# Two-layer hybrid decoder, one core: the expert loop with the down product one expert later and whole gate and up matrices

## The chip, the cores and the metric

One core of a Trainium2 chip runs the whole program. The metric is the time of one execution in microseconds (us), the median of several runs. A profile of one execution gives the spans, waits and transfers below.

## What is computed

Two layers on x of 512 tokens by 1024 columns, all float32: a mixer (state-space and sparse attention in layer 0, block attention in layer 1), and after each mixer a mixture of experts. The mixture is the part that matters here:

```python
h = rms_norm(x, ffn_norm[i])
# router: one of 4 groups, then 2 of its 8 experts per token; 32 experts
def expert_block(args):
    xblk, e = args
    hid = jax.nn.silu(xblk @ w_gate[e]) * (xblk @ w_up[e])
    return hid @ w_down[e]
y = jnp.zeros_like(xt).at[row_token].add(yb * row_weight[:, None].astype(yb.dtype))
x = x + y
```

Each expert has w_gate and w_up of 1024 x 512 and w_down of 512 x 1024, 2 MiB each, so 6 MiB per expert, 32 experts in each of two layers, 384 MiB in all.

## The kernel before

**The expert loop.** Every expert serves up to 64 tokens (CAP). All 32 experts run in order, whatever the router chose. The five engines each run their own program of the loop (`per_expert`, L2059) and meet at semaphores. For expert c TensorE runs, in this order: `gate_up` (L2016, the products at L1951) in two halves over the rows of the matrices; `x_turn` of expert c+1 (four transposes, L1939); two of three passes that pick the rows of expert c+2 out of the tokens (`pick_begin`, L1924); `hid_turn` (two transposes, L1957); the third pass (`pick_end`); and `down` (L2028, the products at L1964). ScalarE computes the silu (L2043), copies the picked rows (L1935) and copies the result out of PSUM (`y_out`, L2048). VectorE multiplies with the up half (L2053), copies the turned hidden rows (L2057) and applies the norm's gain (L1943). GpSimd scatters each expert's result into y_d in DRAM (L1970). The result of expert 31 is not scattered: TensorE adds it at the end from SBUF (L2278).

**The weights.** Three slots (RING = 3) in SBUF each hold the three matrices of one expert. The sync engine's queue (SP) loads them in `moe_sp` (L2104), and its order is the order of the transfers. A gate or up matrix comes as two halves of 1 MiB (`one_half`, L1894, rows of the program at L1897), four rows (8 KB) to a partition; w_down comes in one transfer of 2 MiB (L1906). For c from 0 to 28 `next_weights` (L2127) loads expert c+3 into the slot of c:

```python
                sp.wait_ge(S(f"{t}_guh"), c + 1 + L * NE)
                half_weights(sp, t, L, c + RING, u, 0)
                sp.wait_ge(S(f"{t}_gu"), c + 1 + L * NE)
                half_weights(sp, t, L, c + RING, u, 1)
                sp.wait_ge(S(f"{t}_dn"), c + 2 + L * NE)
                down_weights(sp, t, L, c + RING, u)
```

The semaphore m_guh says that the first half of gate/up is done, m_gu the second, m_dn the down product.

**The end of a layer.** When the scatters of experts 0 to 30 have landed (`fence`, L2076), SP fetches y_d back in four transfers (L2147). VectorE weighs and adds each (`add_fetched`, L2476), then adds expert 31's part (`add_last`, L2483), which gives x for the next layer, or for the output.

**Ahead of the loop.** The normed tokens are split in three bf16 parts: the high part by ScalarE (`high_part`, L663), the rest by VectorE (`rest_part`, L754), middle and low parts at L760 and L769. The last tile is also kept whole (`norm_last`, L675).

Of the kernel before, what the change touches and what calls it, by code (L numbers as in the profile page):

```python
# [81 lines left out]
RING = 3  # L82
# [116 lines left out]
def build(nc, ins, out):  # L199
    ctx = ExitStack()  # L200
    with ctx:
# [379 lines left out]

        def outproj_pe(pe, att, tag, mixT, wo, L):
# [69 lines left out]
        def outproj_act(act, tag, L):  # L652
# [8 lines left out]
            def high_part(i):  # L661
                act.wait_ge(S("norm_rstd"), NT * ORDER[nt] + i + 1)
                nc.scalar.activation(parts[0][i], xt[:, i, :], ACT.Copy, scale=rstd[:, i:i + 1]).then_inc(S("m_hi"), 1)  # L663
# [11 lines left out]
            nc.scalar.activation(norm_last, xt[:, NT - 1, :], ACT.Copy, scale=rstd[:, NT - 1:NT]).then_inc(S("m_norm_last"), 1)  # L675
# [74 lines left out]
        def rest_part(dve, L, i):  # L750
# [3 lines left out]
            nc.vector.scalar_tensor_tensor(rows[:, i, :], xt[:, i, :], rstd[:, i:i + 1], parts[0][i], ALU.mult,  # L754
                                           ALU.subtract).then_inc(S("m_rest"), 1)
# [1137 lines left out]

        def one_half(sp, t, layer, e, u, n, h):  # L1894

            src = ins[("moe_w_gate", "moe_w_up")[n]][layer, bass.ds(e, 1), h * 512:(h + 1) * 512].rearrange("e (p j) f -> p e (j f)", j=4)
            sp.dma_start(wgu[u][:, n, 4 * h:4 * h + 4].rearrange("p (e j) f -> p e (j f)", e=1), src).then_inc(S(f"{t}_{('wgu', 'wgv')[h]}{u}"), 16)  # L1897

        def half_weights(sp, t, layer, e, u, h):

            for n in range(2):
                one_half(sp, t, layer, e, u, n, h)

# [90 lines left out]
        def pick_begin(pe, t, c):  # L1994
            pe.wait_ge(S(f"{t}_ones"), c + 1)
            pe.wait_ge(S(f"{t}_rows"), c + 1)
            pick_rows(range(2))

        def pick_end(pe, t, c):
            pick_rows(range(2, 3)).then_inc(S(f"{t}_picked"), 1)  # L2000

        def picked(pe, t, c):
            pick_begin(pe, t, c)
            pick_end(pe, t, c)
# [11 lines left out]
        def gate_up(pe, t, c, cu, u):  # L2016
# [4 lines left out]
            pe.wait_ge(S(f"{t}_wgv{u}"), 32 * (cu + 1))  # L2021
# [50 lines left out]

        def uses(u):
# [30 lines left out]
        def moe_sp(sp, L, mixed, att):  # L2104
            t, x = "m", f"mx{L}"
            if L == 0:
                for n in range(2):
                    sp.dma_start(row_gain[:, n], ins["ffn_norm"][n].rearrange("(h p j) -> p h j", h=2, j=4)).then_inc(S("gain_in"), 16)
# [18 lines left out]
            def next_weights(c, u):  # L2127
# [428 lines left out]
```

## Time and profile before

| | us |
|---|---|
| median of 3 runs (lowest, highest) | 1636.38 (1635.76, 1638.82) |
| the profiled execution | 1636.7 |
| its span, first to last instruction | 1634.6 |
| TensorE matmul busy | 1577.5 (97%) |
| VectorE, ScalarE, GpSimd busy | 484.7, 360.8, 197.6 |
| moved by all transfers | 474.21 MB |

The span is what the profile measures between its first and last instruction; the remaining 2.1 us of the profiled execution lie around it. "Busy" of TensorE counts overlapping matmuls once. In the profile's timeline a row gives the start, the length, the engine, the line, the operation and, in brackets, how long the engine stood idle before it and what ended that. SPq is the sync engine's queue; a row there is the issue of a transfer and not its delivery. Layer 0's expert loop begins at 326.6 us, layer 1's at 1155.7 us.

### The profile page before, as it was taken

What the parts mean: (1) busy time and instruction counts of PE and PEld (TensorE: products, weight loads), DVE (VectorE), ACT (ScalarE), POOL (GpSimd) and SP (SyncE); (2) the same over time, 40 slices, a digit from 0 to 9 for tenths busy, and PEclk for the clock granted to TensorE, in tenths of its full rate; (3) what the DMA queues carried; (4) which work ended last, traced back from release to release, by engine and by line L of the source; (5) the groups of instructions that cost most, each with busy time, mean ns of one, the idle gap of its engine ahead of it and who ended that gap; (6) DMA issues with size and microseconds to landing.
All of it is one profiled execution on the core that took longest, in us unless ns stands there. A gap on an engine that the chain in (4) does not pass through costs nothing.

```text
span 1634.6 us, 21323 instructions
## 1 busy us (share of the span) xinstructions
PE 1577.5 (97%) x8068; PEld 738.3 (45%) x8072; DVE 484.7 (30%) x1252; ACT 360.8 (22%) x853; POOL 197.6 (12%) x298
## 2 busy tenths in 40 slices
PE   7999989999999999999799999999999999999995
PEld 4545664543333333333445468855433333333332
DVE  1485851531111111111514125734511111111114
ACT  2354461311111111111200246732111111111110
POOL 2240320000000000000102022420000000000000
PEclk9999999999999999999999999999999999999999
DMA  8620127389999999999933320052899999999997
GB/s 244 258 103 7 54 55 308 124 345 420 423 421 421 422 422 422 422 422 419 353 50 104 142 56 1 2 235 78 345 421 421 421 422 421 422 421 422 422 422 310
DMA packets 118314, 474.21 MB, mean 290 GB/s; under 512 B 40822, under 2 KB 47222, under 8 KB 68333
## 3 DMA queue, kind: packets, MB, share of 16 engines
q1 hardware_dynamic: 110156, 456.98, 69.8%
q10 hardware_dynamic: 3136, 8.40, 1.3%
q0 software_dynamic: 4960, 8.04, 1.3%
q8 instruction: 36, 0.59, 0.2%
q14 instruction: 26, 0.21, 0.0%
HBM read 454.84 MB, written 26.77 MB: 295 GB/s over the span
## 4 chain that ended last, share of the span: by engine, by line
PE 67%; SPq 12%; DMA 4%; DVE 3%; issue 1%; ACT 1%; POOL 0%; DVEq 0%; POOLq 0%
PE bank L1951 19%; SPq L1897 10%; PE bank L1964 9%; PE bank L1543 8%; PE bank L1924 8%; PE bank L597 7%; DMA arena<-in_moe_w_up 3%; PE bank L409 3%; PE bank L444 3%; PE bank L1939 2%; SPq L1906 2%; PE bank L426 2%; PE bank L1957 1%; DVE arena L2476 1%; PE bank L458 1%
## 5 line engine op out<-in xcount | busy, mean ns | idle before, releaser
L1951 PE MATMUL bank<-arena 128*64 128x512 f32 x2048 | 451.4, 592 | 6.3 <-DMA arena<-in_moe_w_up 5.9
L1951 PEld LDWEIGHTS bank<-arena 128*64 128x64 f32 x2048 | 143.6, 137 | 302.1 <-issue 291.0
L1964 PE MATMUL bank<-arena 128*64 128x512 f32 x1024 | 230.6, 592 | 2.1 <-DVE arena L2057 2.1
L2053 DVE TENSOR_TENSOR arena<-arena,bank 128x256 f32<-128x256 f32 x64 | 27.0, 422 | 637.2 <-ACT arena L2043 637.1
L1970 POOL DMA_INDIRECT y_d<-arena,slot_row x62 | 60.7, 979 | 857.9 <-ACT arena L2048 830.7
L1924 PE MATMUL bank<-arena 128*64 128x512 bf16 x1272 | 160.1, 381 | 0.2
L1543 PE MATMUL bank<-arena 128*128 128x512 f32 x320 | 139.1, 593 | 0.8 <-ACT arena L321 0.8
L1964 PEld LDWEIGHTS bank<-arena 128*64 128x64 f32 x1024 | 71.9, 137 | 124.1 <-issue 110.5
L2043 ACT ACTIVATE arena<-bank 128x256 f32<-128x256 f32 x64 | 24.6, 384 | 410.5 <-PE bank L1951 410.5
L597 PE MATMUL bank<-arena 128*128 128x512 f32 x256 | 111.8, 594 | 0.0
L895 PE MATMUL bank<-arena 128*128 128x512 f32 (+1 forms) x288 | 105.3, 525 | 0.0
L1543 PEld LDWEIGHTS bank<-arena 128*128 128x128 f32 x320 | 60.1, 190 | 74.3 <-issue 73.3
L1924 PEld LDWEIGHTS bank<-arena 128*64 128x64 bf16 x1272 | 66.8, 109 | 55.5 <-issue 1.2
L1935 ACT ACTIVATE gain<-bank 128x512 f32<-128x512 f32 x64 | 38.2, 597 | 223.5 <-PE bank L1924 222.2
L2048 ACT ACTIVATE arena<-bank 128x512 f32<-128x512 f32 x64 | 38.3, 599 | 190.4 <-PE bank L1964 190.4
L895 PEld LDWEIGHTS bank<-arena 128*128 128x128 f32 x288 | 49.8, 190 | 54.5 <-issue 54.5
L536 DVE CUSTOM_DVE_ANT_0 arena<-bank,arena 128x512 f32<-128x512 f32 (+3 forms) x128 | 52.3, 415 | 72.4 <-PE bank L409 57.5
L597 PEld LDWEIGHTS bank<-arena 128*128 128x128 f32 x256 | 47.9, 190 | 57.1 <-issue 57.1
L409 PE MATMUL bank<-arena 128*128 128x31 f32 (+8 forms) x256 | 67.0, 396 | 0.9 <-ACT arena L1189 0.9
L444 PE MATMUL bank<-arena 128*128 128x128 f32 x384 | 60.8, 281 | 2.2 <-DVE arena L506 1.7
L1939 PEld LDWEIGHTS bank<-ident,gain 128*128 128x128 f32 x256 | 35.9, 210 | 49.6 <-issue 48.7
L2057 DVE COPY arena<-bank 128x256 f32<-128x256 f32 x64 | 27.2, 425 | 89.2 <-PE bank L1957 88.9
(319 smaller groups left out, 1505.0 us busy)
## 6 DMA issues: line engine op xcount, KB each, us to landing
arena<-in_moe_w_gate SPq DMA_DIRECT2D x128, 1024.0 KB, 20.2
arena<-in_moe_w_up SPq DMA_DIRECT2D x128, 1024.0 KB, 23.0
arena<-in_moe_w_down SPq DMA_DIRECT2D x62, 2048.0 KB, 23.3
arena<-in_even_w_in SPq DMA_DIRECT2D x4, 2048.0 KB, 8.4
y_d<-arena ACTq DMA_DIRECT2D x2, 4096.0 KB, 16.8
arena<-y_d SPq DMA_DIRECT2D x8, 1024.0 KB, 9.3
arena<-bias_row_d SPq DMA_DIRECT2D x2, 3584.0 KB, 11.9
arena<-in_odd_w_in SPq DMA_DIRECT2D x3, 2048.0 KB, 14.2
```

The lines of the kernel that those rows point to most:

```text
L409: mm = nc.tensor.matmul(score_bank[u["a"] % 4][:, 0:u["L"]], u["q"], u["k"], start=True, stop="mask" not in u)
L444: mm = nc.tensor.matmul(bank[4 + u["m"] % 2][:, u["b"] * D:(u["b"] + 1) * D], self.pT[0:w, u["a"] % 2, kt, :], u["v"](kt), start=(kt == 0) ...
L536: ins_ = nc.vector.tensor_tensor_reduce(out=self.p[:, u["a"] % 4, 0:L], in0=score_bank[u["a"] % 4][:, 0:L], in1=u["bias"], scale=-1.0, sca ...
L597: mm = nc.tensor.matmul(mix_bank(n)[:, :], mixT[:, k, i * P:(i + 1) * P], wo[half][:, k, :], start=(k == 0), stop=(k == KD - 1))
L895: mm = nc.tensor.matmul(o, l, r, start=(k == 0), stop=(k == KD - 1))
L1543: mm = nc.tensor.matmul(o, lhs(k), rhs(k), start=(k == 0), stop=(k == KD - 1))
L1897: sp.dma_start(wgu[u][:, n, 4 * h:4 * h + 4].rearrange("p (e j) f -> p e (j f)", e=1), src).then_inc(S(f"{t}_{('wgu', 'wgv')[h]}{u}"), 16)
L1924: mm = nc.tensor.matmul(bank[4][h * CAP:(h + 1) * CAP, :], pick[:, i, :], parts[part][i][:, h * 512:(h + 1) * 512], start=(part == 0 and i ...
L1939: mm = nc.tensor.transpose(bank[0][:, j * P:(j + 1) * P], xe[:, j::4], ident[:])
L1951: mm = nc.tensor.matmul(bank[1][fh * CAP:(fh + 1) * CAP, :], xeT[:, j, half * CAP:(half + 1) * CAP], wgu[u][:, :, n, fh * FH:(fh + 1) * FH ...
L1964: mm = nc.tensor.matmul(bank[3][dh * CAP:(dh + 1) * CAP, :], hidT[:, j, fh * CAP:(fh + 1) * CAP], wd[u][:, n, dh * 512:(dh + 1) * 512], st ...
L1970: return nc.gpsimd.indirect_dma_start(out=y_d[layer][:, :], out_offset=bass.IndirectOffsetOnAxis(ap=slot_row[:, n:n + 1], axis=0), in_=yb[ ...
```

## The change

Three things are changed.

1. TensorE runs the down product of expert c-1 right behind gate/up of expert c, and the three passes of picking are together again (`picked`). For the first expert there is no down product ahead, and expert 30's down product (after == 1) and expert 31's run behind their own hid_turn as before. ScalarE's `y_out` moves along.
2. SP loads gate and up of experts 6 to 29 whole, 2 MiB in one transfer, eight rows (16 KB) to a partition, after m_gu (`whole_weights`). Experts 0 to 5, 30 and 31 keep their halves. The down matrix of expert c+2 is now asked for after the gate and up matrices of expert c+3.
3. So that eight consecutive rows can lie on a partition, the columns of the normed tokens are stored in another order: ScalarE and VectorE read x by `by_cols` and write by `by_rows`; `rest_part` becomes two VectorE instructions of 512 columns instead of one of 1024.

```diff
+        def by_cols(ap):
+            return ap.rearrange("t (p h j) -> t h p j", h=2, j=4)
+        def by_rows(ap):
+            return ap.rearrange("t (h p j) -> t h p j", h=2, j=4)
...
-                nc.scalar.activation(parts[0][i], xt[:, i, :], ACT.Copy, scale=rstd[:, i:i + 1]).then_inc(S("m_hi"), 1)
+                nc.scalar.activation(by_rows(parts[0][i]), by_cols(xt[:, i, :]), ACT.Copy, scale=rstd[:, i:i + 1]).then_inc(S("m_hi"), 1)
...
-            nc.vector.scalar_tensor_tensor(rows[:, i, :], xt[:, i, :], rstd[:, i:i + 1], parts[0][i], ALU.mult,
-                                           ALU.subtract).then_inc(S("m_rest"), 1)
+            for h in range(2):
+                ins_ = nc.vector.scalar_tensor_tensor(by_rows(rows[:, i, :])[:, h], by_cols(xt[:, i, :])[:, h], rstd[:, i:i + 1],
+                                                      by_rows(parts[0][i])[:, h], ALU.mult, ALU.subtract)
+            ins_.then_inc(S("m_rest"), 1)
...
+        def whole_weights(sp, t, layer, e, u):
+
+            for n in range(2):
+                src = ins[("moe_w_gate", "moe_w_up")[n]][layer, bass.ds(e, 1)].rearrange("e (p j) f -> p e (j f)", j=KD)
+                sp.dma_start(wgu[u][:, n].rearrange("p (e j) f -> p e (j f)", e=1), src).then_inc(S(f"{t}_wgu{u}"), 16)
...
-            def next_weights(c, u):
+            def next_weights(c, u, halved):
+                if not halved:
+                    sp.wait_ge(S(f"{t}_gu"), c + 1 + L * NE)
+                    whole_weights(sp, t, L, c + RING, u)
+                    next_down(c - 1, (u - 1) % RING)
+                    return
                 sp.wait_ge(S(f"{t}_guh"), c + 1 + L * NE)
                 half_weights(sp, t, L, c + RING, u, 0)
                 sp.wait_ge(S(f"{t}_gu"), c + 1 + L * NE)
...
                     sp.dma_start(wd[2][:, 3, :], down[1][:, 1]).then_inc(S("m_wdq"), 16)
+                else:
+                    next_down(c - 1, (u - 1) % RING)
+
+            def next_down(c, u):
                 sp.wait_ge(S(f"{t}_dn"), c + 2 + L * NE)
                 down_weights(sp, t, L, c + RING, u)
             for u in range(RING):
-                next_weights(u, u)
+                next_weights(u, u, True)
             with sp.Fori(1, TRIPS - 1) as it:
                 for u in range(RING):
-                    next_weights(it * RING + u, u)
+                    next_weights(it * RING + u, u, False)
             for u in range(NE - RING * TRIPS):
-                next_weights(RING * (TRIPS - 1) + u, u)
+                next_weights(RING * (TRIPS - 1) + u, u, True)
+            next_down(NE - RING - 1, (NE - RING - 1) % RING)
...
             def body(e, c, cu, u, after):
-                gate_up(pe, t, c, cu, u)
-                if isinstance(c, int) and c == L * NE:
+                opening = isinstance(c, int) and c == L * NE
+                gate_up(pe, t, c, cu, u, in_halves(L, e, u))
+                if not opening and after >= 1:
+                    down(pe, t, c - 1, cu - (u == 0) + L * (uses((u - 1) % RING) - uses(u)), (u - 1) % RING)
+                if opening:
...
                 if after >= 1:
                     x_turn(pe, t, c + 1)
-                if after >= 2:
-                    pick_begin(pe, t, c + 2)
                 hid_turn(pe, t, c)
                 if after >= 2:
-                    pick_end(pe, t, c + 2)
+                    picked(pe, t, c + 2)
+                else:
+                    down(pe, t, c, cu, u)
                 if isinstance(c, int) and c == L * NE + 2:
                     pe.wait_ge(S("m_wdq"), 32 * (L + 1))
-                down(pe, t, c, cu, u)
```

**SP's queue at the end of a layer's loads.** Before: w_down of expert 30, then gate and up of expert 31 in halves, then its w_down:

```order
L1906 DMA arena<-in_moe_w_down 128x2x2048 [waits m_dn]
L1897 DMA arena<-in_moe_w_gate 128x2048 [waits m_guh]
L1897 DMA arena<-in_moe_w_up 128x2048
L1897 DMA arena<-in_moe_w_gate 128x2048 [waits m_gu]
L1897 DMA arena<-in_moe_w_up 128x2048
L1906 DMA arena<-in_moe_w_down 128x2x2048 [waits m_dn]
```

After the change, the same place: w_down of expert 29 (L1925), gate and up of expert 31, and then w_down of experts 30 and 31:

```order
L1925 DMA arena<-in_moe_w_down 128x2x2048 [waits m_dn]
L1906 DMA arena<-in_moe_w_gate 128x2048 [waits m_guh]
L1906 DMA arena<-in_moe_w_up 128x2048
L1906 DMA arena<-in_moe_w_gate 128x2048 [waits m_gu]
L1906 DMA arena<-in_moe_w_up 128x2048
L1925 DMA arena<-in_moe_w_down 128x2x2048 [waits m_dn] x2
```

Before, expert 30's down matrix stood ahead of expert 31's gate and up; now it stands behind all four of them.

**TensorE at experts 30 and 31, after the change** (L1970 is gate/up, L1983 the down product, L1958 x_turn, L1976 hid_turn, L2280 the transposes of the last expert's weights; m_wd2, m_wd0 and m_wd1 are the down matrices of experts 29, 30 and 31):

```order
L1970 MATMUL bank<-arena 64x512 [waits m_wgv0]
L1970 MATMUL bank<-arena 64x512 x7
L1983 MATMUL bank<-arena 64x512 [waits m_wd2,m_y,m_hT]
L1983 MATMUL bank<-arena 64x512 x7
L1958 MATMUL bank<-ident,gain 128x128 [waits m_xT,m_rows]
L1958 MATMUL bank<-ident,gain 128x128 x3
L1976 MATMUL bank<-ident,arena 128x128 [waits m_hid]
L1976 MATMUL bank<-ident,arena 128x128
L1983 MATMUL bank<-arena 64x512 [waits m_wd0,m_y,m_hT]
L1983 MATMUL bank<-arena 64x512 x7
L2280 MATMUL bank<-ident,arena 128x128 [waits y_gated]
L1970 MATMUL bank<-arena 64x512 [waits m_wgu1,m_hid,m_xT]
```

Expert 29's down product has moved behind gate/up of expert 30; expert 30's own stands, as before, ahead of gate/up of expert 31.

## Rows read from the trace of the kernel before

**Rows 1.** The page: DMA rate and share in 40 slices of the span.

```profile
DMA  8620127389999999999933320052899999999997
GB/s 244 258 103 7 54 55 308 124 345 420 423 421 421 422 422 422 422 422 419 353 50 104 142 56 1 2 235 78 345 421 421 421 422 421 422 421 422 422 422 310
```

**Rows 2.** The page: costliest group, busy us, mean ns | idle before it, releaser.

```profile
L1951 PE MATMUL bank<-arena 128*64 128x512 f32 x2048 | 451.4, 592 | 6.3 <-DMA arena<-in_moe_w_up 5.9
```

**Rows 3.** Timeline of TensorE, one expert in mid-loop, and the next one's start.

```profile
501.93 7.03 PE L1951 MATMUL bank<-arena 128*64 128x512 f32 x32
...
512.74 3.60 PE L1964 MATMUL bank<-arena 128*64 128x512 f32 x16
...
516.17 7.03 PE L1951 MATMUL bank<-arena 128*64 128x512 f32 x32
```

**Rows 4.** Timeline of TensorE, experts 29 (its down), 30 and 31, layer 0.

```profile
758.37 3.60 PE L1951 MATMUL bank<-arena 128*64 128x512 f32 x16
762.50 3.65 PE L1951 MATMUL bank<-arena 128*64 128x512 f32 x16 [0.53 <-DMA arena<-in_moe_w_up]
...
768.15 3.65 PE L1964 MATMUL bank<-arena 128*64 128x512 f32 x16 [0.55 <-DVE arena L2057]
...
773.13 3.65 PE L1951 MATMUL bank<-arena 128*64 128x512 f32 x16 [0.74 <-DMA arena<-in_moe_w_up]
778.15 3.65 PE L1951 MATMUL bank<-arena 128*64 128x512 f32 x16 [1.38 <-DMA arena<-in_moe_w_up]
...
783.83 3.65 PE L1964 MATMUL bank<-arena 128*64 128x512 f32 x16 [0.52 <-DVE arena L2057]
```

**Rows 5.** Timeline, all engines, the scatter and the fetch at layer 0's end.

```profile
773.21 0.97 POOL L1970 DMA_INDIRECT y_d<-arena,slot_row  x1 [12.28 <-ACT arena L2048]
...
779.74 2.58 SPq L2147 DMA_DIRECT2D arena<-y_d  x4
...
785.83 5.25 DVE L2476 SCALAR_TENSOR_TENSOR arena<-arena,other_w 128x1024 f32<-128x1024 f32 x4 [2.06 <-DMA arena<-y_d]
...
791.11 1.28 DVE L2483 TENSOR_TENSOR arena<-arena,bank 128x512 f32<-128x512 f32 x2
```

**Rows 6.** Timeline, all engines, layer 1's end.

```profile
1603.20 0.97 POOL L1970 DMA_INDIRECT y_d<-arena,slot_row  x1 [12.55 <-ACT arena L2048]
1608.15 3.65 PE L1951 MATMUL bank<-arena 128*64 128x512 f32 x16 [1.38 <-DMA arena<-in_moe_w_up]
1609.83 2.60 SPq L2147 DMA_DIRECT2D arena<-y_d  x4
```

**Rows 7.** Timeline of SP's queue, the first loads of layer 0's loop.

```profile
345.42 0.38 SPq L1906 DMA_DIRECT2D arena<-in_moe_w_down  x1
...
366.54 0.33 SPq L1897 DMA_DIRECT2D arena<-in_moe_w_gate  x1
...
373.92 0.38 SPq L1906 DMA_DIRECT2D arena<-in_moe_w_down  x1
```

**Rows 8.** One stretch: us, busy per engine, clock, DMA share, GB/s.

```profile
346.00:349.00 3.00, 3.00 (x16) 0.98 (x14) 0.00 (x0) 0.08 (x1) 1.28 (x1) 1.00 0.86 238
```

**Rows 9.** Stretches with transfers of 2 KB rows, then of 8 KB rows.

```profile
62.00:78.00 16.00, 16.00 (x42) 6.84 (x41) 12.73 (x17) 8.95 (x17) 8.18 (x6) 1.00 1.01 420
...
255.00:280.00 25.00, 25.00 (x59) 11.02 (x58) 2.75 (x4) 2.89 (x8) 0.00 (x0) 1.00 1.01 425
...
260.00:265.00 5.00, 5.00 (x13) 2.19 (x12) 0.69 (x1) 0.72 (x2) 0.00 (x0) 1.00 1.02 433
```

**Rows 10.** Timeline ahead of layer 0's loop: VectorE, ScalarE, TensorE.

```profile
321.28 1.28 DVE L754 SCALAR_TENSOR_TENSOR arena<-arena,rstd 128x1024 f32<-128x1024 f32 x1
...
316.51 1.13 ACT L675 ACTIVATE gain<-arena,rstd 128x1024 f32<-128x1024 f32 x1
...
323.25 1.02 PE L2214 MATMUL bank<-gain,arena 128*64 128x512 f32 x4
```

More of the change, by code:

```diff
@@ L674, in outproj_act @@
                     middle_part(act, L, i)
-            nc.scalar.activation(norm_last, xt[:, NT - 1, :], ACT.Copy, scale=rstd[:, NT - 1:NT]).then_inc(S("m_norm_last"), 1)
+            nc.scalar.activation(by_rows(norm_last), by_cols(xt[:, NT - 1, :]), ACT.Copy, scale=rstd[:, NT - 1:NT]).then_inc(S("m_norm_last"), 1)
             middle_part(act, L, NT - 1)
@@ L1892, in build, with some_rows @@
         x_row_f, x_no_row = at(EW + 1024, 1), at(EW + 1025, 1)
+        def some_rows(sp, dst, layer, e, n, a, b):
+            src = ins[("moe_w_gate", "moe_w_up")[n]][layer, bass.ds(e, 1)].rearrange("e (p j) f -> p e j f", j=KD)
+            return sp.dma_start(dst.rearrange("p (e j) f -> p e j f", e=1), src[:, :, a:b])
         def one_half(sp, t, layer, e, u, n, h):
-            src = ins[("moe_w_gate", "moe_w_up")[n]][layer, bass.ds(e, 1), h * 512:(h + 1) * 512].rearrange("e (p j) f -> p e (j f)", j=4)
-            sp.dma_start(wgu[u][:, n, 4 * h:4 * h + 4].rearrange("p (e j) f -> p e (j f)", e=1), src).then_inc(S(f"{t}_{('wgu', 'wgv')[h]}{u}"), 16)
+            some_rows(sp, wgu[u][:, n, 4 * h:4 * h + 4], layer, e, n, 4 * h, 4 * h + 4).then_inc(S(f"{t}_{('wgu', 'wgv')[h]}{u}"), 16)
         def half_weights(sp, t, layer, e, u, h):
@@ L1992, in ones_for, with picked @@
             pick_ones(e).then_inc(S(f"{t}_ones"), 1)
-        def pick_begin(pe, t, c):
+        def picked(pe, t, c):
             pe.wait_ge(S(f"{t}_ones"), c + 1)
             pe.wait_ge(S(f"{t}_rows"), c + 1)
[L1997 to L2004, printed above, removed]
+            pick_rows().then_inc(S(f"{t}_picked"), 1)
         def rows_out(act, t, c):
@@ L2014, in x_turn, with gate_up @@
             turn_rows().then_inc(S(f"{t}_xturn"), 1)
-        def gate_up(pe, t, c, cu, u):
+        def gate_up(pe, t, c, cu, u, halved):
             pe.wait_ge(S(f"{t}_xT"), c + 2)
@@ L2020, in gate_up @@
             gate_up_mms(u, 0).then_inc(S(f"{t}_guh"), 1)
-            pe.wait_ge(S(f"{t}_wgv{u}"), 32 * (cu + 1))
+            pe.wait_ge(S(f"{t}_wgv{u}"), 32 * halved)
             gate_up_mms(u, 1).then_inc(S(f"{t}_gu"), 1)
@@ L2071, in per_expert, with in_halves @@
                 one(RING * TRIPS + u, TRIPS, u, NE - 1 - RING * TRIPS - u)
+        def in_halves(L, e, u):
+            had = L * (2 + (u < NE - RING * TRIPS))
+            if isinstance(e, int):
+                return had + min(e // RING + 1, 2) + (e >= RING * TRIPS)
+            return had + 2
         def uses(u):
@@ L2107, in moe_sp @@
                 for n in range(2):
-                    sp.dma_start(row_gain[:, n], ins["ffn_norm"][n].rearrange("(h p j) -> p h j", h=2, j=4)).then_inc(S("gain_in"), 16)
+                    sp.dma_start(row_gain[:, n], ins["ffn_norm"][n].rearrange("(p h j) -> p h j", h=2, j=4)).then_inc(S("gain_in"), 16)
             else:
@@ L2295, in body @@
                     rows_out(act, t, c + 1)
+                elif after >= 1:
+                    if isinstance(c, int) and c == L * NE + 1:
+                        act.wait_ge(S(f"{t}_routed"), past("m_routed") + L + 1)
+                    y_out(act, t, c - 1, (u - 1) % RING)
                 if after >= 2:
                     rows_out(act, t, c + 2)
-                if isinstance(c, int) and c == L * NE:
-                    act.wait_ge(S(f"{t}_routed"), past("m_routed") + L + 1)
-                y_out(act, t, c, u)
+                else:
+                    y_out(act, t, c, u)
                 if after == 1:
```

## The prediction

> **What bounds the kernel now.** I read the page's slices first, then TensorE's timeline in the loop and at its end, then the chain of work behind the end. In the slices the transfer engines are full (share 9, 419 to 423 GB/s) through nearly all of both expert loops [rows 1]. TensorE looks full too: one expert takes 516.17 - 501.93 = 14.24 us without a gap [rows 3]. Which of the two decides? The page charges only 5.9 us of waiting to the weights [rows 2], which would make the transfers harmless. The loop's end says otherwise. Each half of a gate/up pair (2 MiB) lets TensorE start when it has landed: the last two starts are 773.13 and 778.15, each after a wait for w_up [rows 4], so 2 MiB take 5.02 us when the transfers are the limit, and 6 MiB 15.1 us, more than the 14.24 us that TensorE needs. The three slots give a head start of two experts and more, the transfers lose about 0.8 us of it (1.1 with the scatters) per expert, and around expert 30 it is used up. So TensorE is the bound up to expert 29 and **the transfers set when a layer ends**: what matters in this change is how many bytes stand ahead of the matrix for which TensorE waits at the end, and how fast they move.
>
> Behind the weights stands a second chain: expert 30's down product (768.15), its scatter (773.21), the landing and the fetch (779.74), VectorE's first addition (785.83), its four in a row, the addition of expert 31's part (791.11) [rows 4, 5]. Layer 1 has the same steps at 1603.20 and 1609.83 [rows 6]. Whatever delays expert 30's down product delays the layer.
>
> **The change part by part.**
>
> *The order in SP's queue at the end.* Before, expert 30's w_down stood ahead of expert 31's gate and up. Now it is the last but one, with 4 MiB of expert 31 in front of it, yet TensorE still needs it ahead of gate/up 31. The bytes up to and with it are those that before ended with the last up half: it lands when that half did, at 778.15, if rate and start stay. Before, its product started at 768.15. That is +10.0 us on the start, in layer 0, and 1608.15 - (1603.20 - 5.06) = 10.0 in layer 1, where 5.06 is the step from product to scatter in layer 0 (773.21 - 768.15) [rows 4 to 6].
>
> *The release of the slots.* Down c-1 behind gate/up c starts gate/up of all later experts 3.43 us earlier, and a whole matrix waits for m_gu and not for m_guh. From expert 1 on the halves are asked for as before, but w_down of expert 5, asked for at 373.92 before [rows 7], now comes behind gate/up of expert 6, which is asked for when gate/up 3 ends: at 373.7 + 6.9 - 3.4 = 377.2. The transfers stood idle before 346, and 238 GB/s over 3 us [rows 8] puts their start at 349 - 3 x 238/422 = 347.3, 1.9 us after the issue at 345.42. Six pieces of 2 MiB issued up to 366.54 [rows 7] last until 347.3 + 6 x 5.02 = 377.4, up to 0.8 more with the scatters between them. The next bytes come at 377.2 + 1.9 = 379.1. The transfers stand idle for 0.9 to 1.7 us; I take 1.0. One expert later there is a margin (394.4 against 393.4) which grows from there. **+1.0 us per layer**, bounds 0 and 2.5 (the margin missed once more).
>
> *The rate of whole matrices.* 24 experts x 2 pieces of 2 MiB, 241 us at 5.02 us, now go in rows of 16 KB. The trace has no such load. Nearest: rows of 2 KB moved at 420 GB/s, rows of 8 KB at 425 with no scatter beside them [rows 9]. Over 16 engines these are 78.0 and 308.4 ns a row, so 1.2 ns per row and the rest by the byte; at 16 KB it makes 425.8 GB/s, +0.2%. **-0.5 us per layer.** Bounds: 0, and -4.6 if the best five microseconds (433 GB/s [rows 9], 1.9% over 425) became the rule. I take the row fit, since four times the row size brought only 1.2%.
>
> The Trainium skill, page "DMA: Bandwidth & Descriptors", section "Bandwidth", speaks for a larger gain: it gives 341 GB/s for a transfer of 1 MB and 425 for 16 MB, and asks for large transfers. Its section on the anatomy of one DMA puts a fixed 2 us on each. By that rule, an estimate, halving the transfers of a gate/up pair would save 4 us per expert. The trace disagrees: two 1 MiB transfers in a row land in 5.02 us, which is the full rate, so no fixed time is left between them.
>
> *The down product one expert later.* TensorE does the same products: 14.24 us stays, less at most 0.1 of gaps. Nothing of it reaches the end while the transfers set it. Gate/up 30 would start at 754.9, 3.4 us early, and stand before w_down of 30 at about 767; it waits there some 11 us for 778.65.
>
> *Columns rearranged.* Four times per layer one VectorE instruction of 1.28 us becomes two of some 0.69 us (+0.1), and ScalarE reads in pieces of four. VectorE's last one is at 321.28 and ScalarE's last copy ends at 317.6, while TensorE asks for that copy at 323.25 [rows 10]: 5.6 us of cover. The middle and low parts of the last tile are asked for after gate/up 0. Zero; if strided access doubled both, still below the cover for ScalarE, and at most 0.3 us for VectorE.
>
> **The sum.** Per layer: +10.0 + 1.0 - 0.5 = +10.5 us on expert 30's down product, on the scatter and on the issue of the fetch. In the fetch a little comes back: before, its first part landed 6.1 us after issue, behind the last w_down, which landed about 783.2; now that matrix lands at 783.7 and the fetch is issued at 790.2 into empty engines. I take 5.6 us in place of 6.1 (bounds 4.5 and 6.2), -0.5. Expert 31's part is no new wait: 778.65 + 3.65 + 0.7 + 6.9 + 2.0 + 3.65, plus 2.4 for the copy and the last product, gives 798, and VectorE asks for it at 801.1. So +10.0 us per layer, **+20.0 us in all**. The profiled execution took 1636.7 us, 0.3 above the median: 1656.7 against it, **1656.4 us** as a median.
>
> **Rivals.**
> 1. *Partly repaid by the rate.* Whole matrices run at about 433 GB/s. -4.6 in place of -0.5 per layer: 1648 us. For: single stretches show it [rows 9]. Against: 30 us means in the loops never do [rows 1]. The skill's page (section "Where 436 GB/s comes from") has 435 GB/s as the ceiling of the ports; at that the time, an estimate, would be 1646.
> 2. *Faster: the transfers cease to be the limit.* If 16 KB rows were 4.2% faster (about 443 GB/s; 10.0 of 241 us), w_down 30 would land by 768.15; that is the point from which it decides. Beyond it TensorE rules: its product starts at 754.9 + 6.9 + 3.4 + 1.1 = 766.5, 1.6 us earlier than before, and up to 0.1 us for each of 30 experts: 1627 to 1633. For: the number of transfers and of rows falls by two fifths and a third. Against: no row of the trace reaches that rate over more than 2 us.
> 3. *The starvation repeats.* Between two issues up to 10.8 us pass now, 7.4 before. If the 1.9 us of start were paid for every whole expert until the backlog holds, say five times per layer: +18, 1672 us.
> 4. *The change doesn't bind:* w_down of 30 is not late, because the backlog at the end is smaller than I read, and gains and losses cancel: 1636. Against: the waits of experts 30 and 31 [rows 4].
>
> **How the numbers follow.** Forecast 0.73, rival 1 0.13, rival 2 0.07, rival 3 0.04, rival 4 0.03. A change of 0.2% (3.3 us) is about what a measurement of this kernel can tell from none. Faster 0.07, within it 0.03, slower 0.90. Range: low end 1656.4 - 8.2 (rate) - 2.0 (no idle) - 2.2 (quick fetch) = 1644; high end +3.0 (idle 2.5) + 1.0 (no gain of rate) + 1.2 (fetch 6.2) = 1661.6. I set 1643 to 1662, which takes in rival 1 and leaves out about 2 in 10.
>
> **What would show it.** In the profile after: TensorE waits once per layer for w_down, for 8 to 12 us, ahead of expert 30's down product, near 778.7 and 10 us after its old place in layer 1; the two short waits for w_up at expert 31 are gone. Whole matrices at 422 to 426 GB/s in the slices. A dip of the DMA share near 378. The scatter at 783.7, the fetch at 790. The forecast is wrong if the slices show over 430 GB/s, if the share dips in more than one place early in the loop, or if w_down 30 is there when TensorE asks.

## The result, and the profile after

| | before | after |
|---|---|---|
| median in us (lowest to highest, 4 runs each) | 1637.48 (1635.76 to 1638.82) | 1646.85 (1645.33 to 1647.82) |
| ratio of the times, 95% interval | | 1.0057 (1.004 to 1.0074) |
| the profiled execution, and its span | 1636.7, 1634.6 | 1645.33, 1643.6 |

The changed kernel is slower by 9.4 us, 0.57%. The sign was forecast, the size was not: +20 us was the sum, and the time lies inside the range, near its quick end.

The page of the changed kernel, transfers in 40 slices and the two groups of products (L1970 is gate/up, L1983 the down product; the same rows of before are [rows 1] and [rows 2]):

```profile
DMA  7620217399999999998923320062899999999995
GB/s 243 256 102 7 73 35 307 141 376 411 426 424 427 426 425 427 428 424 358 328 40 115 129 56 1 2 255 80 351 407 427 425 428 425 425 426 427 425 422 233
...
L1970 PE MATMUL bank<-arena 128*64 128x512 f32 x2048 | 451.1, 593 | 14.2 <-DMA arena<-in_moe_w_up 13.7
...
L1983 PE MATMUL bank<-arena 128*64 128x512 f32 x1024 | 234.9, 601 | 22.7 <-DMA arena<-in_moe_w_down 21.7
```

Two things are to be seen. The loops run at 424 to 428 GB/s where they ran at 421 to 423, about 1% more. And the down product now waits 21.7 us for w_down. The view of waits shows that these are two waits only, one in each layer (columns: engine, line, releaser, us in total, times, longest):

```profile
PE bank L1983 <- DMA arena<-in_moe_w_down: 21.7, 2, 10.9
PE bank L1970 <- DMA arena<-in_moe_w_up: 13.7, 13, 1.3
```

The timeline at the end of layer 0 (what was [rows 4, 5]) and of layer 1 ([rows 6]), and four stretches (columns as in [rows 8], the granted clock, the share and the rate of the transfers last):

```profile
773.83 5.39 PE L1983 MATMUL bank<-arena 128*64 128x512 f32 x16 [10.90 <-DMA arena<-in_moe_w_down]
...
780.63 0.97 POOL L1989 DMA_INDIRECT y_d<-arena,slot_row  x1 [16.24 <-ACT arena L2060]
...
783.09 2.65 SPq L2176 DMA_DIRECT2D arena<-y_d  x4
...
788.36 0.42 DVE L2069 COPY arena<-bank 128x256 f32<-128x256 f32 x1 [0.60 <-PE bank L1976]
...
789.48 5.25 DVE L2510 SCALAR_TENSOR_TENSOR arena<-arena,other_w 128x1024 f32<-128x1024 f32 x4 [0.69 <-issue]
...
794.76 1.28 DVE L2517 TENSOR_TENSOR arena<-arena,bank 128x512 f32<-128x512 f32 x2
...
1616.38 0.97 POOL L1989 DMA_INDIRECT y_d<-arena,slot_row  x1 [16.61 <-ACT arena L2060]
...
1619.03 2.68 SPq L2176 DMA_DIRECT2D arena<-y_d  x4
```

```profile
760.00:780.00 20.00, 9.10 (x38) 3.53 (x36) 3.92 (x11) 1.34 (x3) 0.97 (x1) 0.74 0.73 305
374.00:377.00 3.00, 3.00 (x16) 0.84 (x12) 0.42 (x1) 0.38 (x1) 0.00 (x0) 1.00 0.83 279
...
770.00:772.00 2.00, 0.00 (x0) 0.00 (x0) 0.00 (x0) 0.00 (x0) 0.00 (x0) 0.50 0.84 352
...
778.00:780.00 2.00, 2.00 (x12) 0.77 (x10) 0.00 (x0) 0.74 (x2) 0.00 (x0) 1.00 0.00 0
```

The long wait stands ahead of expert 30's down product, as forecast. Three things beside it were not. The product behind the wait takes 5.39 us (5.90 in layer 1) and not 3.65, with a mean granted clock of 0.74 over 760 to 780. The scatter lands 2.46 us after its issue (783.09 - 780.63; 2.65 in layer 1), where it had needed 6.53 [rows 5]; from 778 to 780 nothing at all is moved. And VectorE's first addition is not released by the fetch: it follows the copy of expert 31's hidden rows (788.36).

**The ledger.** All of it is counted from the start of a layer's expert loop, which is 324.18 and 1159.46 after the change and 326.56 and 1155.69 before. The start in layer 0 is 2.4 us earlier, and I don't count that as the change's: of the runs below that share the changed kernel's work ahead of the loop, some start at 324.5 to 324.6 (e1, e7, e9, e10), some at 326.2 to 326.6 (e6, e8, e11) and one at 329.0 (e2).

| step, us against before | forecast | layer 0 | layer 1 |
|---|---|---|---|
| start of down product 30 (773.83 - 324.18, and so on) | +10.5 | +8.1 | +7.2 |
| its start to the scatter's issue (5.06 before; 6.80, 7.30) | 0 | +1.7 | +2.2 |
| scatter to fetch (6.53, 6.63 before; 2.46, 2.65) | 0 | -4.1 | -4.0 |
| fetch to first addition (6.09, 6.22 before; 6.39, 5.96) | -0.5 | +0.3 | -0.3 |
| sum, up to `add_last` | +10.0 | +6.0 | +5.2 |

Both layers give 11.2 us; 0.2 lies between and behind the loops, 2.4 come off for the earlier start: 9.0 us, the difference of the spans. So 2.4 us of what the measurement lies below the forecast belong to a start that varies between these runs, and not to the change: that part is luck.

### The profile page after: what moved, and what is told of

Same layout as the page of the kernel before. It is cut to its first block, busy times and chain, and to the rows that moved or that the text cites. A ratio compares the mean times of both kernels' runs of the same rounds, so it can differ in the third digit from the quotient of the medians.

```text
span 1643.6 us, 21102 instructions
## 1 busy us (share of the span) xinstructions
PE 1563.5 (95%) x8072; PEld 744.8 (45%) x8072; DVE 485.8 (30%) x1260; ACT 360.7 (22%) x853; POOL 197.2 (12%) x298
## 4 chain that ended last, share of the span: by engine, by line
PE 79%; DMA 13%; DVE 3%; SPq 2%; ACT 1%; issue 1%; DVEq 0%; POOL 0%; ACTq 0%
PE bank L1970 21%; PE bank L1983 9%; DMA arena<-in_moe_w_up 9%; PE bank L1552 8%; PE bank L1943 8%; PE bank L604 7%; PE bank L904 6%; DMA arena<-in_moe_w_down 4%; PE bank L409 3%; PE bank L444 3%; SPq L1906 2%; PE bank L1958 2%; PE bank L426 2%; PE bank L985 2%; DVE arena L2510 1%
## 5 line engine op out<-in xcount | busy, mean ns | idle before, releaser
L1970 PE MATMUL bank<-arena 128*64 128x512 f32 x2048 | 451.1, 593 | 14.2 <-DMA arena<-in_moe_w_up 13.7
L1970 PEld LDWEIGHTS bank<-arena 128*64 128x64 f32 x2048 | 146.5, 137 | 285.2 <-issue 265.8
L1983 PE MATMUL bank<-arena 128*64 128x512 f32 x1024 | 234.9, 601 | 22.7 <-DMA arena<-in_moe_w_down 21.7
L1983 PEld LDWEIGHTS bank<-arena 128*64 128x64 f32 x1024 | 75.3, 139 | 169.3 <-issue 167.8
L1962 DVE TENSOR_TENSOR arena<-bank,row_gain 128x512 f32<-128x512 f32 x64 | 44.3, 692 | 197.0 <-PE bank L1958 197.0
L1938 DVE TENSOR_TENSOR arena<-arena,slots 128x256 bf16<-128x256 f32 x64 | 27.2, 425 | 116.9 <-PE bank L1943 116.7
```

The costliest lines, as they stand in the source:

```text
L1962: return nc.vector.tensor_tensor(xeT.rearrange("p j (h s) -> p j h s", h=2), split(bank[0][:, :], 4, 2, CAP), row_gain[:, L].rearrange("p ...
L1970: mm = nc.tensor.matmul(bank[1][fh * CAP:(fh + 1) * CAP, :], xeT[:, j, half * CAP:(half + 1) * CAP], wgu[u][:, :, n, fh * FH:(fh + 1) * FH ...
L1983: mm = nc.tensor.matmul(bank[3][dh * CAP:(dh + 1) * CAP, :], hidT[:, j, fh * CAP:(fh + 1) * CAP], wd[u][:, n, dh * 512:(dh + 1) * 512], st ...
```

## The experiments

All times are medians, with the ratio to the kernel before on the same chip. "Loop to addition" is the time from the loop's start to VectorE's first `add_last`, layer 0 and layer 1; before has 464.6 and 465.7, the changed kernel 470.6 and 470.8.

**The queue's order** (e1_tail_order). In SP's queue w_down 30 again stands ahead of gate/up 31.

```diff
-            for u in range(NE - RING * TRIPS):
-                next_weights(RING * (TRIPS - 1) + u, u, True)
-            next_down(NE - RING - 1, (NE - RING - 1) % RING)
+            next_weights(NE - RING - 2, 0, True)
+            next_down(NE - RING - 2, 0)
+            sp.wait_ge(S(f"{t}_guh"), NE - RING + L * NE)
+            half_weights(sp, t, L, NE - 1, 1, 0)
+            sp.wait_ge(S(f"{t}_gu"), NE - RING + L * NE)
+            half_weights(sp, t, L, NE - 1, 1, 1)
+            next_down(NE - RING - 1, 1)
```

> Only SP's order at each layer's end differs from the changed kernel: w_down of expert 30 is issued ahead of gate and up of expert 31. Late-matrix theory (the loss is TensorE's 10.9 and 10.8 us of waiting for w_down 30 and what hangs on it): w_down 30 lands some 10 us earlier, about 763.7 in layer 0, the wait falls to about 1 us, the scatter goes out near 769 and VectorE's last additions start near 781 to 782 in place of 789.5; minus 8 us per layer, about 1631 us, which is faster than before. Rival, starvation in the loop (the later release of whole matrices costs the time): the order at the end changes nothing that matters, 1645 to 1647 us. Rival, columns: the same 1645 to 1647.

Measured: 1636.3 us, ratio 1.0004 (0.9994 to 1.0014). Its timeline:

```profile
763.68 3.65 PE L1983 MATMUL bank<-arena 128*64 128x512 f32 x16 [0.88 <-DVE arena L2069]
...
770.90 0.97 POOL L1989 DMA_INDIRECT y_d<-arena,slot_row  x1 [6.62 <-DMA y_d<-arena,slot_row]
...
777.39 2.72 SPq L2180 DMA_DIRECT2D arena<-y_d  x4
...
782.79 2.60 DVE L2514 SCALAR_TENSOR_TENSOR arena<-arena,other_w 128x1024 f32<-128x1024 f32 x2 [3.56 <-DMA arena<-y_d]
```

The loss is gone, so the order in the queue is its cause. The product starts 439.2 us behind the loop's start (763.68 - 324.46), 10.4 before the changed kernel's 449.65, near the forecast's +10.0. Here it waits for the copy of its own hidden rows (L2069) and not for weights, so this is what the product moved and not the matrix; e5_rows_8k below tests the forecast's arithmetic. Yet only 5.7 us of it reach the addition (464.9; 466.4 in layer 1). Weights are in flight again (268 GB/s over 771 to 777), the scatter needs 6.5 us again (770.90 to 777.39), and one thing is new: GpSimd issues it only when expert 29's scatter has landed, which is the wait of 6.62 in the row. I had counted neither when I expected 1631 us; it became 1636. e9_scatter_pair tests the second.

**All in halves** (e2_halves). The changed kernel with gate and up of all experts in halves of 1 MiB, `next_weights(..., True)` everywhere.

> The changed kernel with all gate and up matrices in halves of 1 MiB (rows of 8 KB); the order of TensorE and of the queue stays changed. If rows of 16 KB (or fewer transfers) raise the rate from 421.5 to 425.5 GB/s as the slices of the changed kernel suggest, this loses 241 us x 0.95% = 2.3 us per layer and wins back the 1 us of idle near 375: about +1.3 to +2.3 per layer, 1649.5 to 1651.5 us, slices back at 421 to 422. If the rate has nothing to do with it (row fit of the prediction, +0.2%): minus 1 per layer from the idle, 1645 to 1647.

Measured: 1652.84 us, ratio 1.0096 (1.0075 to 1.0117), some 6 us over the changed kernel and 1.3 over what I expected. From loop to addition it has 473.4 us in both layers, 2.8 and 2.6 more than the changed kernel. The transfers fall back to the rate of before (the page's slices), and TensorE waits 17 times for w_down, 40.0 us in all:

```profile
GB/s 235 261 102 7 52 56 305 128 356 421 422 422 421 421 422 422 422 422 388 303 63 100 143 55 2 2 235 80 367 421 421 421 421 422 422 423 421 422 422 230
```

**Whole matrices alone** (e3_whole_alone). The kernel before with rearranged columns and whole matrices for experts 6 to 29, but TensorE's and SP's order as before.

> The kernel before with the columns rearranged and the matrices of experts 6 to 29 whole; the down product and the order of the queue stay as before. Late-matrix theory: no loss, the rate gain of about 2 us per layer removes the waits for w_up of experts 30 and 31, 1633 to 1636 us, slices at 425. Rival, starvation or the columns cost the time: slower than 1637.5, up to 1647.

Measured: 1635.95 us, ratio 1.0003 (0.9993 to 1.0012).

```profile
771.58 0.97 POOL L1985 DMA_INDIRECT y_d<-arena,slot_row  x1 [11.51 <-ACT arena L2063]
...
778.10 2.64 SPq L2175 DMA_DIRECT2D arena<-y_d  x4
...
783.40 2.60 DVE L2504 SCALAR_TENSOR_TENSOR arena<-arena,other_w 128x1024 f32<-128x1024 f32 x2 [3.67 <-DMA arena<-y_d]
...
787.47 2.60 DVE L2504 SCALAR_TENSOR_TENSOR arena<-arena,other_w 128x1024 f32<-128x1024 f32 x2 [1.47 <-DMA arena<-y_d]
```

A higher rate alone gains nothing. The waits of TensorE for w_up are gone, but in before's order its down product 30 has no weights to wait for, and TensorE's own program sets it (441.9 us behind the start, before 441.6). The additions now wait for the fetch twice, 3.67 and 1.47 us. It also clears this part of the change of the loss.

**Columns alone** (e4_columns_alone). The kernel before with `by_cols` and `by_rows` and the split `rest_part`; a half is now four of the eight rows of each partition.

> The kernel before with the columns rearranged and nothing else: two VectorE instructions in place of one for each last part, strided ScalarE copies, gate and up still in halves of 1 MiB, each row now 8 KB of a 16 KB stretch in memory. My theory (the columns cost nothing, since TensorE asks for them 5.6 us later): within 0.1% of the kernel before, 1634 to 1638 us, slices at 421 to 423 GB/s as before. Rival (rows of 8 KB taken out of stretches of 16 KB move at another rate): slices off by 0.5% or more, and 2 to 4 us either way.

Measured: 1636.24 us, ratio 0.9991 (0.9981 to 1.0001), 464.6 and 465.5 from loop to addition, and the loops' slices stay at 421 to 422 GB/s. The columns cost nothing, and rows of 8 KB taken out of stretches of 16 KB move as before.

**Whole transfers in rows of 8 KB** (e5_rows_8k).

```diff
-                src = ins[...][layer, bass.ds(e, 1)].rearrange("e (p j) f -> p e (j f)", j=KD)
+                src = ins[...][layer, bass.ds(e, 1)].rearrange("e (h p j) f -> p (e h) (j f)", h=2, j=4)
```

> The changed kernel with the old split of rows over partitions: a whole matrix still goes in one transfer of 2 MiB, but in rows of 8 KB (two per partition), with the columns as they were before. It tells whether the rate came from the longer rows or from the fewer transfers. Row theory (the 0.95% come from rows of 16 KB instead of 8): slices at 421 to 423 GB/s instead of 425 to 428, and a time near that of the run with all halves, 1651 to 1653 us. Transfer theory (fewer and larger transfers are faster, whatever their rows): slices at 425 or more and 1645 to 1648 us.

Measured: 1654.51 us, ratio 1.0104 (1.0087 to 1.0121). The page's slices:

```profile
GB/s 241 255 102 7 71 36 305 140 369 409 422 422 421 422 421 422 422 423 369 320 46 108 134 55 1 2 265 82 352 406 421 422 422 421 422 423 422 422 422 222
```

The row theory holds, though the time is 1.5 us over the 1651 to 1653 that it gave. Whole transfers in rows of 8 KB move at 421 to 423 GB/s, as halves do; fewer transfers bring nothing, and the 1% comes from the 16 KB rows. This run also tests the arithmetic of the forecast without its rate term: its product 30 starts 452.2 us behind the loop's start, and the forecast's 441.6 + 10.0 (order) + 1.0 (idle) is 452.6. Against it the changed kernel's 449.65 gives what the long rows are worth at that place: 2.5 us. In layer 1 the same product starts 454.2 us behind the loop's start (1619.41 - 1165.19), where the forecast's terms without the rate give 442.45 + 11.0 = 453.45 and the changed kernel has 449.62: 4.6 us for the long rows. Against e2_halves, which moves at the same rate (451.5 and 452.2), it also prices the later release of whole matrices: 0.7 us in layer 0 and 2.0 in layer 1.

**A busy wait** (e6_busy_wait). The changed kernel with 46 products into an unused bank ahead of expert 30's down product, so that TensorE does not stand still while it waits.

```diff
+                    if after == 1:
+                        for _ in range(46):
+                            nc.tensor.matmul(bank[6][:, :], identb[:], parts[2][0][:, 0:512], start=True, stop=True)
                     down(pe, t, c, cu, u)
```

> The changed kernel with 46 matmuls (512 columns, bf16, about 9.8 us) into a free bank ahead of expert 30's down product, inside the wait of 10.9 us. Nothing else changes. If the idle wait costs a second time through the clock (down product 5.4 and 5.9 us in place of 3.65), this removes it: down product back to 3.65 us, minus 1.7 and 2.2 us, about 1643 us. If the clock is not the reason, the down product stays at 5.4 to 5.9 us and the time at 1646 to 1647.

Measured: 1644.23 us, ratio 1.0048 (1.0032 to 1.0063). That is 2.6 us less than the changed kernel by the medians and 1.5 by the ratios, whose intervals overlap, so the reading rests on the traces. One stretch, and the timeline in layer 1:

```profile
760.00:780.00 20.00, 19.05 (x90) 7.75 (x86) 4.34 (x12) 0.98 (x2) 0.97 (x1) 1.00 0.85 352
```

```profile
1610.23 3.65 PE L1983 MATMUL bank<-arena 128*64 128x512 f32 x16 [0.92 <-DMA arena<-in_moe_w_down]
...
1615.29 0.97 POOL L1989 DMA_INDIRECT y_d<-arena,slot_row  x1 [14.44 <-ACT arena L2060]
...
1617.94 2.66 SPq L2176 DMA_DIRECT2D arena<-y_d  x4
```

With the engine busy its clock stays at 1.00 and the product takes 3.65 us; the scatter comes 1.6 and 1.4 us earlier, counted from the loop's start (454.9 and 455.5 against 456.5 and 456.9). In the changed kernel the granted clock stood at 1.00 over 764 to 766, at 0.78 over 766 to 768, at 0.50 (1.2 GHz) from 768 to 776 and at 0.66 over 776 to 778, in the idle stretch and in the first products behind it. That costs about 1.5 us per layer.

**The down product last** (e7_down_last). On TensorE, expert 30's down product too goes behind the next gate/up, that of expert 31; ScalarE's part moves along.

```diff
-                if not opening and after >= 1:
+                if not opening:
                     down(pe, t, c - 1, ...)
...
-                else:
+                elif after == 0:
                     down(pe, t, c, cu, u)
```

> The changed kernel with one more step of the same shift: the down product of expert 30 stands behind gate/up of expert 31 on TensorE (and its scaling by ScalarE with it), SP's queue unchanged. My theory: the wait of 10.9 us is not paid in full, because TensorE does gate/up 31 in part of it; w_down 30 lands at the same time, but TensorE's clock has not fallen, so the product takes 3.65 us again instead of 5.4 and 5.9, and what follows it (scatter, landing in 2.5 us, fetch) comes early by that, and expert 31's own down product no longer keeps VectorE: 1.7 to 3.5 us per layer, 1640 to 1643 us. Rival: if the order on TensorE is what costs (gate/up 31 now ahead of the product for which the scatter waits, 6.9 us, with its second half waiting for w_up), the product starts later than w_down's landing and the time is 1647 or more.

Measured: 1645.83 us, ratio 1.0057 (1.004 to 1.0073), the same as the changed kernel.

```profile
767.05 8.78 PE L1970 MATMUL bank<-arena 128*64 128x512 f32 x32
...
775.67 3.60 PE L1983 MATMUL bank<-arena 128*64 128x512 f32 x16
...
780.69 0.97 POOL L1989 DMA_INDIRECT y_d<-arena,slot_row  x1 [16.01 <-ACT arena L2060]
...
785.18 2.66 SPq L2176 DMA_DIRECT2D arena<-y_d  x4
...
790.61 5.25 DVE L2510 SCALAR_TENSOR_TENSOR arena<-arena,other_w 128x1024 f32<-128x1024 f32 x4 [10.44 <-DMA arena<-y_d]
```

The long wait is gone, and the two layers differ. In layer 0 the clock falls all the same: TensorE stands idle for 3.25 us ahead of the transposes at 766.47, the granted clock is 0.97 over 766 to 768, 0.50 over 768 to 770 and 0.68 over 770 to 772, and gate/up 31 takes 8.78 us in place of 7.09. The product then starts 451.1 us behind the loop's start, 1.4 later than in the changed kernel, and the scatter is issued at 456.1 against 456.5. In layer 1 the same 3.25 us of idle leave the clock at 1.00, gate/up 31 takes 7.09 us, the product starts at 449.4 and the scatter goes out at 454.4 against 456.9: the gain of my theory, in this layer alone.

This gain is then lost: the scatters took 4.5 and 4.3 us to the fetch's issue, although the transfer engines had as little to do as in the changed kernel, where they took 2.5 and 2.7. In the changed kernel all 80 packets of the scatter have moved by 783.1. Here 75 of 80 have moved by 783.0, and the last five, all small, follow between 783.5 and 785.2; in layer 1 the last six follow in the same way, up to 1619. What held them back I did not find.

One more detail: the first addition now starts 5.43 us after the fetch (before the change 6.09, in the changed kernel 6.39), so in the changed kernel VectorE was held by the copy for expert 31's hidden rows and not by the fetch.

**The shift alone in the right order** (e8_order_halves). The first run with all matrices in halves, as in e2_halves.

> The shift of the down product alone, with w_down 30 put ahead of gate/up 31 in SP's queue and all gate/up matrices in halves of 1 MiB, no whole matrix: against the first run (same order, whole matrices, 1636.3 us) it prices the rate where the queue's order is right; against the run with all halves (1652.8) it prices the order. Theory that the order explains the loss: 1637 to 1641 us, slices at 421 to 423 GB/s, no wait of TensorE over 3 us for w_down at expert 30. Rival (the shift itself, by releasing the buffers later, costs whatever the order at the end): 1645 or more, with many short waits for w_down in the loop.

Measured: 1640.59 us, ratio 1.003 (1.0019 to 1.0041); loop to addition 466.8 and 468.3, TensorE waits 15 times for w_down, 18.3 us in all. The order explains most: against e2_halves it is 0.66% of the kernel before, 11 us. But the shift with halves is still slower than the kernel before, by 2.3 and 2.6 us per layer. With long rows (e1_tail_order) the same order comes out even. The rest is GpSimd's wait for expert 29's scatter to land: here expert 30's scatter goes out 7.05 us behind the start of its product. In e10_pair_halves, the same kernel without that wait, it is 5.07, and the addition comes at 464.7 and 465.8, as before the change.

**The scatter not waiting** (e9_scatter_pair). The first run, and GpSimd issues expert 30's scatter without waiting for that of expert 29 to land.

```diff
                 scatter_y(t, L, e % RING, e)
+                if e == NE - 3:
+                    continue
                 pool.wait_ge(S(f"{t}_yout"), 16 * (L * (NE - 1) + e + 1))
-                pool.sem_inc(S(f"{t}_yfree"), 1)
+                pool.sem_inc(S(f"{t}_yfree"), 2 if e == NE - 2 else 1)
```

> The first run (w_down 30 ahead of gate/up 31) and besides POOL issues the scatter of expert 30 without waiting for that of expert 29 to land, which in that run held it from 767.9 or so to 770.9 and took 6.6 us under load; it waits for both afterwards. Theory (that landing of the second last scatter, and not the weights, is what the end waits for once the order is right): the scatter of expert 30 is issued 1.5 to 2.2 us earlier, the fetch and the additions with it, 3 to 4 us in two layers: 1632 to 1633.5 us. Rival (the transfer engines serve the scatters one behind the other and behind the weights, so an earlier issue lands no earlier): 1636 us, landing time longer by what the issue was earlier.

Measured: 1628.71 us (1627.94 to 1631.29), ratio 0.9953 (0.9936 to 0.9969): faster than both kernels.

```profile
769.13 0.97 POOL L1989 DMA_INDIRECT y_d<-arena,slot_row  x1 [4.47 <-ACT arena L2060]
...
775.63 2.71 SPq L2180 DMA_DIRECT2D arena<-y_d  x4
...
781.89 5.25 DVE L2516 SCALAR_TENSOR_TENSOR arena<-arena,other_w 128x1024 f32<-128x1024 f32 x4 [2.08 <-DMA arena<-y_d]
```

Counted from the loop's start, the scatter is issued 1.9 us earlier than in e1_tail_order (2.9 in layer 1) and still lands in 6.5 (6.7), with the scatter of expert 29 still in flight when it is issued. All four additions then run in a row, where there was a gap of 1.3 us (1.2), but they start 0.9 us (0.8) later behind the fetch. Together that is 2.3 and 3.3 us less from loop to addition (462.6 and 463.1), 5.6 in all where I expected 3 to 4: the scatter of layer 1 gained more than I had counted. By the ratios it is 8 us less than e1_tail_order; what the other 2 to 3 us are, I did not take apart.

**The same in halves** (e10_pair_halves).

> The fastest run so far (w_down 30 ahead of gate/up 31, the scatter of expert 30 not waiting for that of 29; 1628.7 us) with all gate and up matrices in halves of 1 MiB: what the rate of the whole matrices is worth once order and scatter are right. Theory (the weights still bound the loop): 4 to 6 us more, 1633 to 1635 us, with over ten waits for w_down or w_up in each layer's loop. Rival (with the shift the tail has enough reserve and the rate is worth little): 1629 to 1631 us.

Measured: 1636.03 us, ratio 0.9995 (0.9985 to 1.0005), 464.7 and 465.8 from loop to addition, 15 waits for w_down and 18.6 us in them. By the ratios (0.9953 and 0.9995) the whole matrices are worth 7 us here, where the end no longer hides them; from loop to addition it is 4.9 us (2.1 and 2.8). Alone (e3_whole_alone) they were worth nothing. I had expected over ten waits in each layer's loop; there are fewer, 15 for w_down and 4 for w_up in both layers together.

**The scatter under load** (e11_loaded_scatter). The changed kernel with 4 MiB more to load behind w_down 31.

```diff
             next_down(NE - RING - 1, (NE - RING - 1) % RING)
+            sp.wait_ge(S(f"{t}_gu"), NE - 2 + L * NE)
+            for n in range(2):
+                src = ins[("moe_w_gate", "moe_w_up")[n]][L, NE - 3:NE - 2].rearrange("e (p j) f -> p e (j f)", j=KD)
+                sp.dma_start(wgu[2][:, n].rearrange("p (e j) f -> p e (j f)", e=1), src).then_inc(S("gain_in"), 16)
...
             fetch(lambda i: f"{t}_yin{i}")
+            sp.wait_ge(S("gain_in"), 32 * (L + 2))
```

> The changed kernel with 4 MiB of loads more at the end of each layer (gate and up of expert 29 once more, into the slot that it has left), queued behind w_down 31, so that the transfer engines are still full when expert 30's scatter is issued at 780.6. In the changed kernel that scatter landed in 2.46 us on engines with nothing to do; in the kernel before, under load, 6.53. My theory (the load on the transfer engines sets the landing): landing 6 to 7 us, fetch issued 4 us later than in the changed kernel, first addition 3.5 to 5 us later, in two layers: 1653 to 1657 us, which is where my forecast stood. Rival (the scatter's landing does not depend on the loads; it was shorter for another reason): landing 2.5 us, fetch issued as in the changed kernel, its data behind the added loads, 1 to 2 us later, 1648 to 1650 us.

Measured: 1656.56 us, ratio 1.0118 (1.0101 to 1.0135).

```profile
775.93 5.63 PE L1983 MATMUL bank<-arena 128*64 128x512 f32 x16 [10.93 <-DMA arena<-in_moe_w_down]
...
782.97 0.97 POOL L1989 DMA_INDIRECT y_d<-arena,slot_row  x1 [16.49 <-ACT arena L2060]
...
790.97 2.80 SPq L2180 DMA_DIRECT2D arena<-y_d  x4
...
796.32 2.61 DVE L2515 SCALAR_TENSOR_TENSOR arena<-arena,other_w 128x1024 f32<-128x1024 f32 x2 [5.19 <-DMA arena<-y_d]
```

```profile
778.00:781.00 3.00, 3.00 (x12) 0.84 (x8) 0.00 (x0) 0.00 (x0) 0.00 (x0) 0.68 1.02 426
781.00:784.00 3.00, 3.00 (x18) 1.19 (x16) 0.00 (x0) 1.18 (x2) 0.97 (x1) 1.00 0.88 377
```

Down product 30 starts where it did (449.75 us behind the loop's start, against 449.65), and with weights in flight the scatter lands in 8.0 us (8.05 in layer 1) and not in 2.5. So the load makes the landing long, though no load does not always make it short (e7_down_last). I had expected 6 to 7 us. The difference goes with the rows of the weights: over the middle of the loops (400 to 640 and 1240 to 1440) the scatters land in 7.8 to 8.0 us, by the median, in the changed kernel and the runs with 16 KB rows whose landings the profile gives (e1, e3, e6, e7, e11), and in 6.5 to 6.6 in the kernel before and the runs with 8 KB rows (e2, e4, e5, e8, e10). The loads added here are whole matrices. The time is near the forecast's 1656.4, but not term by term: this landing is longer than the 6.5 us of the forecast, and the slow clock is in it too.

## Why the sign was right and the size was not

- **The order in SP's queue: right, place and size.** "That is +10.0 us on the start." With the rate's term out of it, the product starts at 452.2 us where the forecast's terms give 452.6 (e5_rows_8k, layer 0; 454.2 against 453.45 in layer 1). The order alone moved the product by 10.4 us (e1_tail_order against the changed kernel, 449.65 - 439.2).
- **The release of the slots: right.** 279 GB/s over 374 to 377 are 3 x (1 - 279/427) = 1.0 us of idle transfers in layer 0, at the forecast's place and size; layer 1 has one such dip too (291 GB/s over 1210 to 1212). At expert 30's product, e5_rows_8k against e2_halves gives 0.7 us for it in layer 0 and 2.0 in layer 1, inside the bounds of 0 and 2.5.
- **The step that failed: the sum's "+10.5 us on expert 30's down product, on the scatter and on the issue of the fetch".** It let the scatter's landing of 6.5 us stand. That duration was read with weights in flight (346 GB/s between 773 and 780). But the forecast's own first step leaves the engines empty: whatever delays w_down 30 to nearly the last transfer also delays the scatter until nothing else moves. Its own numbers said so, 783.7 for the last weights' landing and 783.7 for the scatter; it drew the conclusion for the fetch and not for the scatter. The landing fell to 2.5 and 2.7 us, -4.1 and -4.0 us. The two layers lie 8.8 us below the forecast's 20 (11.2 measured): -8.1 is this step, and the others (rate and what goes with it -5.7, clock +3.9, fetch +1.0) nearly cancel. e11_loaded_scatter puts a load back, and the landing is long again.
- **The rate: the term was mis-sized.** -0.5 us stood; e5_rows_8k gives -2.5 for layer 0 and -4.6 for layer 1. The row fit took 425 GB/s for rows of 8 KB from a stretch before the loop [rows 9], while the loop itself had 422 [rows 1]; with 16 KB rows it has 424 to 428. Layer 0 lies inside the bound of -4.6 and layer 1 on it. The Trainium skill, page "DMA: Bandwidth & Descriptors", section "Bandwidth", has 341 GB/s for 1 MB and 425 for 16 MB, for transfers issued from GpSimd. These queued transfers of SP don't follow it: whole transfers of 2 MiB in 8 KB rows run at 421 to 423 GB/s, as halves of 1 MiB do. The length of the row made the 1%.
- **The clock: forgotten.** "TensorE does the same products" left out that it does the first of them at half clock after standing idle: +1.7 and +2.2 us up to the scatter. The wait was forecast (8 to 12 us, came as 10.9), what it does to the product behind it was not. e6_busy_wait returns 1.6 and 1.4 of it.
- **The fetch: right by itself, no gain.** 5.6 us stood for it, 6.4 and 6.0 came. "Expert 31's part is no new wait" was checked for `add_last` only; in VectorE's own order the copy for expert 31's hidden rows stands ahead of the first addition. With the fetch at the forecast's 790.2 that copy would have been done in time; with the scatter's quick landing it came too late. e7_down_last, where it comes earlier, has 5.4.
- **TensorE's loop.** It takes 13.93 us per expert (492.30 to 506.23), 0.31 less than [rows 3] and not "at most 0.1". Nothing of it reached the end, as said, since the weights set that: the head start is used up earlier, and from 660.94 (expert 24) and 1481.97 on TensorE waits for w_up at nearly every expert, the 13 waits of the view above.
- **Columns rearranged: zero, right** (e4_columns_alone).

The rivals: *partly repaid by the rate* (1648 us) is nearest in time, but not by its mechanism: it wanted 433 GB/s, 428 was the most a slice had, and more of what was repaid came from the scatter than from the rate. *Faster, the transfers cease to be the limit* did not come, but e9_scatter_pair shows its ground: with the order mended and the scatter free, the shift and the long rows together are 0.5% faster than before. *The starvation repeats* and *the change doesn't bind* fall with the two waits of 10.9 and 10.8 us and the single dip of the rate in each layer, near 375 and 1211.

The -2.4 and -3.3 us between forecast and measurement at down product 30 divide into -2.0 and -4.1 for the rate's term and -0.4 and +0.8 for the rest. Still open: why the scatters of e7_down_last took 4.5 and 4.3 us on idle engines, and why its clock fell in one layer and not in the other.

## What to carry to other kernels

A duration read under load is a duration with that load: when a change moves a step to where other traffic has ended, or begins, price it anew, for the forecast's first step often changes the conditions of the third. When a stage ends with a chain (product, scatter, fetch, addition), mend the order in the queue first, then look which link the mended chain waits for; here the rate of the weights was worth nothing alone and 7 us after two other edits. And a long wait of TensorE costs the wait and a slow product behind it.

## What the runs showed that was not expected

- One indirect scatter of 64 slots lands in 2.5 to 2.7 us on idle transfer engines (in e7_down_last in 4.3 to 4.5). With weights in flight it takes 6.5 to 6.6 us behind rows of 8 KB and 7.8 to 8.0 behind rows of 16 KB, by the median in mid-loop. Issued with another scatter in flight it still lands in 6.5 to 6.7.
- Rows of 16 KB move at 424 to 428 GB/s in the loops, rows of 8 KB at 421 to 423, in transfers of 1 or of 2 MiB alike.
- After 10.9 us of idle TensorE the granted clock stood at 0.50, and the 16 products of expert 30 took 5.3 to 6.4 us (the longest in e2_halves) in place of 3.65; 46 products in the gap prevented it. An idle stretch of 3.25 us was followed by 0.50 in one layer of e7_down_last and by 1.00 in the other.
